# Waiting for a quarter of a weight block instead of the whole block, in a two-block float32 model kernel

## What is computed

```python
# first block
p = h @ w_in                       # "in": 11 weight blocks
...                                # RWKV recurrence, 31-tap convolution
mix = concat([rwkv_out, c]) @ w_out          # "out": 4 blocks
hid = h @ ffn_up                   # "up": 22 blocks, then a 3-tap convolution
f = (gelu(gate) * up) @ ffn_down   # "down": 12 blocks
# second block, layer 0 (latent attention, 512 tokens and 256 context tokens)
q_lat, kv_lat, k_pe, gate = split(t @ w_in)  # "mla_in": 7 blocks
q = (rms_norm(q_lat) @ w_qb)
kv = (rms_norm(kv_lat) @ w_kvb)    # "mla": 4 blocks
...                                # attention of 16 heads, then "mla_out": 4 blocks
# second block, layer 1 (differential attention): "diff" 16 blocks, "diff_out" 4 blocks
```

## Time and profile before

| | us |
|---|---|
| median of 3 runs | 1885.46 |
| lowest, highest | 1881.81, 1889.06 |
| the profiled execution | 1880.98 |
| its span on the core | 1879.2 |
| PE busy | 1767.7 (94%) |
| POOL busy | 961.4 (51%) |
| DVE busy | 1039.4 (55%) |

### The profile page before, as it was taken

One profiled execution on the slowest core, in us unless ns is written; L12 is line 12 of the kernel. 1 busy time (PEld: TensorE's weight loads), 2 busy tenths in 40 slices (PEclk: granted clock), 3 DMA queues, 4 the chain that ended last, 5 costly groups with the idle time before them and its releaser, 6 DMA issues.

```text
span 1879.2 us, 24128 instructions
## 1 busy us (share of the span) xinstructions
PE 1767.7 (94%) x9332; PEld 1398.8 (74%) x9332; DVE 1039.4 (55%) x1285; ACT 749.5 (40%) x1217; POOL 961.4 (51%) x762
## 2 busy tenths in 40 slices
PE   4999999999999999999898899999988999999977
PEld 2777999766578888886687677777846888888766
DVE  4498545366655555102453666666565666666565
ACT  3453767313233333001331565555134444444442
POOL 4353667365179999888155121234623444444062
PEclk8999999799999999999999999999999999999988
DMA  4121000133212232322211100002130111111121
GB/s 180 47 102 54 2 1 2 47 135 135 90 67 89 91 110 89 147 100 104 110 45 50 40 23 1 23 1 90 68 140 29 45 45 47 61 51 46 46 90 45
DMA packets 18715, 126.20 MB, mean 67 GB/s; under 512 B 2080, under 2 KB 2208, under 8 KB 4160
## 3 DMA queue, kind: packets, MB, share of 16 engines
q1 hardware_dynamic: 18048, 121.79, 17.6%
q10 hardware_dynamic: 576, 3.15, 0.5%
HBM read 122.83 MB, written 2.10 MB: 66 GB/s over the span
## 4 chain that ended last, share of the span: by engine, by line
PE 54%; issue 18%; POOL 14%; DVE 9%; ACT 3%; DMA 1%; POOLq 0%; SPq 0%; ACTq 0%; DVEq 0%
POOL w_hi L613 7%; PE banks L1152 4%; POOL cacc L637 4%; PE banks L1131 3%; PE banks L1312 3%; PE banks L1315 3%; PE banks L1313 3%; POOL w_lo L604 3%; PE banks L1013 3%; PE banks L720 3%; PE banks L1018 3%; PE banks L1014 3%; PE banks L1367 2%; PE banks L705 2%; PE banks L707 2%
## 5 line engine op out<-in xcount | busy, mean ns | idle before, releaser
L613 POOL TENSOR_TENSOR w_hi<-raw,der 128x512 fp32r<-128x512 f32 x300 | 347.0, 1167 | 547.5 <-PE banks L1315 210.6
L604 POOL TENSOR_TENSOR w_lo<-raw,w_hi 128x512 fp32r<-128x512 f32 x336 | 470.4, 1412 | 68.1 <-ACT w_hi L1440 68.1
L705 PE MATMUL banks<-h_hi,w_hi 128*128 128x512 f32 x528 | 210.1, 398 | 15.1 <-DVE h_lo L2016 12.6
L707 PE MATMUL banks<-h_hi,w_lo 128*128 128x512 f32 x528 | 206.5, 391 | 0.0
L706 PE MATMUL banks<-h_lo,w_hi 128*128 128x512 f32 x528 | 206.5, 391 | 0.0
L1312 PE MATMUL banks<-h_hi,w_hi 128*128 128x512 f32 (+1 forms) x384 | 147.0, 383 | 4.6 <-DVE h_lo L2496 3.9
L705 PEld LDWEIGHTS banks<-h_hi,w_hi 128*128 128x128 f32 x528 | 99.6, 189 | 43.5 <-issue 12.8
L1313 PE MATMUL banks<-h_lo,w_hi 128*128 128x512 f32 (+1 forms) x384 | 131.1, 356 | 0.0
L1915 ACT ACTIVATE dP<-banks,der 128x768 f32<-128x768 f32 x64 | 57.8, 902 | 167.9 <-DVE der L2529 167.9
L1315 PE MATMUL banks<-h_hi,w_lo 128*128 128x512 f32 (+1 forms) x384 | 116.4, 357 | 0.0
L707 PEld LDWEIGHTS banks<-h_hi,w_lo 128*128 128x128 f32 x528 | 99.7, 189 | 20.9
(11 more groups left out here) (455 smaller groups left out, 4231.1 us busy)
## 6 DMA issues: line engine op xcount, KB each, us to landing
raw<-in_stream SPq DMA_DIRECT2D x84, 1024.0 KB, 4.8
ada_raw<-in_ada_w SPq DMA_DIRECT2D x18, 1024.0 KB, 6.0
raw<-in_ada_w SPq DMA_DIRECT2D x6, 1024.0 KB, 4.8
xT<-in_x_t SPq DMA_DIRECT2D x2, 1024.0 KB, 6.0
xT<-in_x_t SPq DMA_DIRECT2D x1, 2048.0 KB, 7.8
out_t<-z SPq DMA_DIRECT2D x8, 256.0 KB, 2.0
ctxT<-in_ctx_t ACTq DMA_DIRECT2D x1, 1024.0 KB, 4.9
rope<-in_ropes ACTq DMA_DIRECT2D x2, 512.0 KB, 4.3
```

The costliest lines, as they stand in the source:

```text
L604: return pool.tensor_tensor(lo[:, h, part(i), :], raw_tiles(half)[:, part(i), :], hi[:, h, part(i), :], ALU.subtract)
L613: pool.tensor_tensor(hi[:, h, part(i), :], raw_tiles(half)[:, part(i), :], one, ALU.mult).then_inc(hi_done, 1)
L705: pe.matmul(banks[b][:, :], hi, rhs_hi[:, k, :], start=(at_k == 0), stop=False)
L707: mm = pe.matmul(banks[b][:, :], lo, rhs_hi[:, k, :], start=False, stop=(at_k == KT - 1))
```

## The change

A new semaphore `quarter_split` counts the low parts 0, 1 and 2 of every block, three a block. The last low part still counts `split_full`. The function `quarter(n, i)` gives the semaphore and the value that say that quarter i of block n is split. In `project`, the down loop and `mla_in` the wait for `split_full` of the block is replaced by four waits, one ahead of every fourth tile. All other products wait as before. So that the number of semaphores stays in bounds, `lam_exp` of the second layer now reuses `cln_root` with an offset of 1.

```diff
+    quarter_split = sem("quarter_split")
+    def quarter(n, i):
+        return (quarter_split, (PARTS - 1) * n + (i + 1)) if i < PARTS - 1 else (split_full, n + 1)
...
     # POOL, split()
-                    low_of(half, h, i - 1, hi, lo)
+                    low_of(half, h, i - 1, hi, lo).then_inc(quarter_split, 1)
...
     # POOL, input blocks 2 to 10
             for i in range(PARTS):
-                ins = low_of(half_of(n), half_of(n), i)
-            ins.then_inc(split_full, 1)
+                low_of(half_of(n), half_of(n), i).then_inc(quarter_split if i < PARTS - 1 else split_full, 1)
...
     # PE, project()
-            pe.wait_ge(split_full, n + 1)
             for j in range(2):
...
+                    if at_k % 4 == 0:
+                        pe.wait_ge(*quarter(n, 2 * j + at_k // 4))
...
     # PE, down loop
-                pe.wait_ge(split_full, 6 * i + (STREAM["down"] + u + 1))
                 for t in range(TILES):
...
+                    if t % 4 == 0:
+                        pe.wait_ge(*quarter(6 * i + (STREAM["down"] + u), t // 4))
...
     # PE, mla_in()
-                if m % 2 == 0:
-                    pe.wait_ge(split_full, n + 1)
...
-            mm = wide_project(0, 0, KT, m % 2, half_of(n), h2_hi, h2_lo, tile0=KT * (m % 2), ready=None if m else mh_ready, part=part)
+            for k in range(KT) if part is None else part:
+                if k % 4 == 0:
+                    pe.wait_ge(*quarter(n, 2 * (m % 2) + k // 4))
+                mm = wide_project(0, 0, KT, m % 2, half_of(n), h2_hi, h2_lo, tile0=KT * (m % 2), ready=None if m else mh_ready, part=[k])
```

More of the change, by code:

```diff
@@ L469, in build @@
     NL, LAM = 88, 96
-    lam_prod, lam_sum, lam_exp = (sem(n) for n in ("lam_prod", "lam_sum", "lam_exp"))
+    lam_prod, lam_sum = sem("lam_prod"), sem("lam_sum")
+    lam_exp = Later(cln_root, 1)
     o_sq, o_root, o_scaled = (sem(n) for n in ("o_sq", "o_root", "o_scaled"))
@@ L1871, in _ @@
         act.wait_ge(lam_sum, 1)
-        act.activation(der[:, LAM + 2:LAM + 4], banks[4][:, 0:2], ACT.Exp).then_inc(lam_exp, 1)
+        act.activation(der[:, LAM + 2:LAM + 4], banks[4][:, 0:2], ACT.Exp).then_inc(lam_exp.sem, 1)
         low_rows, high_rows = slice(0, 64), slice(64, 128)
@@ L2498, in _ @@
         dve.tensor_tensor(h2_lo[:, KT - 1, :], zh[:, 1, :], h2_hi[:, KT - 1, :], ALU.subtract).then_inc(mh_ready, 1)
-        dve.wait_ge(lam_exp, 1)
+        dve.wait_ge(*lam_exp.at(1))
         chain.link(dve.tensor_scalar(der[:, LAM + 4:LAM + 5], der[:, LAM + 3:LAM + 4], der[:, LAM + 2:LAM + 3], None, ALU.subtract))
```

## The result

The changed kernel takes 1874.36 us (median of 8 runs, 1867.35 to 1878.40) where the kernel before takes 1887.89 (8 runs, 1881.81 to 1889.37). The ratio is 0.993, with an interval of 0.9915 to 0.9945: faster by 0.7%, and the whole interval lies beyond 0.5%. The profiled executions took 1868.69 and 1880.98 us, 12.3 less; the sum of the prediction was 12.5.

The account below looks back on a forecast made before the run. PE bounds the kernel (busy 94% of the span), so only its waits for `w_lo` can go: 4.1 + 6.8 + 1.6 = 12.5 us off the median 1885.46 gives 1873.0 us, range 1867 to 1882.

Parts of the forecast that it names:

- Up and input projection, 0: In the 22 up and 11 input projection blocks PE was not held by POOL's split, so the gain is 0.
- Down projection, 4.1 us: PE's three gaps behind short blocks go whole, with the slow matmul after each: 1.22 + 1.34 + 1.22 + 0.3 us.
- the middle gap: Down projection, at 817.68: 1.34 us counted to POOL's pass, though the view of waits names ACT's queue.
- POOL keeps up: Down projection: three POOL passes take 28 us against PE's 30.0 us for three blocks, so PE runs through.
- The wait at `mla_in(10)`, 6.8 us: End of the latent input projection: the first piece needs only quarter 0, starting at 1000.63 instead of 1007.45.
- The clock behind it, 1.6 us: First tiles of `mla_in(10)`: without PE's idle time they run at full instead of half clock, 1.6 us more won.
- no idle time, no fall: At `mla_in(10)`: without PE's idle time the clock has no cause to fall to half; worth 1.6 us.
- The added waits, 0: 149 more wait executions on PE cost 0, because its queue runs ahead of the matmuls; upper bound 28 us.
- The stall behind `mla_in(11)` moves up and does not shrink: The stall of some 11 us (1033 to 1044.38) starts with DVE's fills after PE's last product and keeps its length.
- Rival (a): The 6.8 + 1.6 us are given back before 1044 through unmoved DVE or POOL work: 1881.4 us; chance 0.13.
- Rival (b), the clock: Half clock stays or moves behind the stall at 1033 to 1044: gain 9.3 us, time 1876.2; chance 0.13.
- The median, 1873.0: Whole kernel: the median of 1885.46 us falls by 12.5 us, 0.66% less; chance 0.65.

Follow-up runs that it names:

- the third experiment: Only the input and up projections wait by quarters, the signals on POOL stay, against the kernel before: 1887.14 us (10 runs), ratio 1.0.
- the first experiment: Only the down projection waits by quarters, the signals on POOL stay, against the kernel before: 1885.32 us (10 runs), ratio 0.9983.
- 3.0 us of idle time: Only the latent input projection waits in parts, by halves of a block instead of the whole block as in the kernel before: 1885.58 us in one run.

## Why the prediction was right, step by step

- **Up and input projection, 0.** Right: 10.88 us a block before and after, and the third experiment at a ratio of 1.0.
- **Down projection, 4.1 us.** Right: 4.2 in the trace (1.22, 1.34, 1.22 at the three gaps, and 0.1 for each slow matmul), 3.2 by the runs with this part alone, whose interval holds 4.1; in that kernel's profile 1.0 us goes to the longer half clock behind the wait at `mla_in(10)`. That the middle gap was POOL's and not ACT's was argued ahead and is shown by the first experiment. POOL keeps up: no late quarter shows in PE's waits.
- **The wait at `mla_in(10)`, 6.8 us.** Right: 10.65 - 3.92 = 6.7, with PE 0.14 behind quarter 0 instead of the 0.06 that were taken.
- **The clock behind it, 1.6 us.** Right in size: 12.23 - 10.65 = 1.6. (The 1.06 us that the prediction calls the fourth tile's is the third's.) That the size fits is in part luck: behind the same wait the clock cost 2.6 us in the profile with the down projection alone. The reason given (no idle time, no fall) holds at this place, and with 3.0 us of idle time left the fall and the whole loss were still there. As a general reason it fails: near 67 us the clock fell without idle time.
- **The added waits, 0.** Right, and far from the edge: in the input and up projections 48 waits a block instead of 4 cost nothing.
- **The stall behind `mla_in(11)` moves up and does not shrink.** Right to 0.02 us (-12.25 before it, -12.27 at 1044). Rival (a) fails: nothing in the stall hangs on work that did not move. What the prediction had wrong is what PE waits for first there: ACT's row, not DVE's fills.
- **Rival (b), the clock.** It did happen, but for other sums than it priced. The stretches lie elsewhere in after (one at 896.7, one at 1023.0, where before they were at 881.1 and 1038.1), and the largest effect was one that the prediction did not see. The stretch behind the stall costs nothing more in after, though it is twice as long. The modulation products behind the down projection ran at full clock in after, so that PE was 6.96 and then 7.9 us ahead, and then it waited (PE and DVE of after, and DVE of before):

```profile
898.29 0.77 PE L1021 MATMUL banks<-h_hi,w_hi 128*128 128x512 f32 x1 [3.69 <-DVE h_lo L2317]
...
897.18 0.96 DVE L2317 TENSOR_TENSOR h_lo<-mh,h_hi 128x768 fp32r<-128x768 f32 x1 [0.98 <-ACT h_hi L1667]
...
901.05 0.96 DVE L2308 TENSOR_TENSOR h_lo<-mh,h_hi 128x768 fp32r<-128x768 f32 x1 [0.99 <-ACT h_hi L1658]
```

  `h_lo` comes 897.18 - 901.05 = -3.87 us against before, what the down projection had won (3.86), and `mla_in(0)` starts with it. DVE's chain sets this place, so what the clock gave to PE in it is given back, in full. A step for the half clock at 881 would have been worth nothing in the sum, in either direction.
- **The median, 1873.0.** 1874.36 was measured. The sum was set against 1885.46, the median of three runs; further runs of that kernel have medians of 1885.6 to 1887.9. Against 1887.89 the sum gives 1875.4, and the difference of the medians is 13.5 us (10.4 to 16.0 by the interval). That the two profiled executions differ by 12.3 is closer than it can be relied on: behind 1400 the difference moves between 10.9 and 13.0 us with the clock.

Open: why the early stretch falls in some executions and not in others, and what the kernel would win if it never came. Whether the 32 and 96 rows bring it is not shown either: two profiles without it, where it falls in seven of twelve, may be chance.

## What to carry to other kernels

Where one engine prepares a block in pieces and another waits for the whole, read the gap at each block start: a gap of 1 us is worth a signal per piece, a near tie in the chain is worth nothing, and further waits that are met in time cost nothing on an engine whose queue has work. Price a removed wait together with the half clock behind it, but do not count on that while some us of the wait are left, expect its size to differ from one profile to the next (1.6 and 2.6 us here), and then look for the next engine's chain at which what was won is given back. Work taken off a critical place belongs into holes of its engine that the timeline shows; moved as one piece to "later" it became the next wait. And an edit that is to keep the clock up has a price of its own, to be read from matmuls at full clock in both kernels.

## What the runs showed of the hardware

- 990 more satisfied waits in the up loop, one ahead of each of 48 matmuls a block, left the starts at 0.226 to 0.227 us.
- The clock fell to half while PE had work without a break: from about 67 us in seven profiles of twelve, in the stretch of products that use 32 or 96 of 128 rows. None of the seven has a gap of PE between 46 and 90 us. This timeline of PE in the profile with the latent part alone shows two products of one form at full and at half clock:

```profile
63.60 1.12 PE L737 MATMUL banks<-Q,gup 96*128 96x512 f32 x2
...
66.82 2.07 PE L737 MATMUL banks<-Q,gup 96*128 96x512 f32 x2
```

  The Trainium skill, "TensorE: Matmul & The Clock Gate", section "HAM oscillation — how this bites in real kernels", names idle gaps of PE as what brings the fall; these traces show a fall without any. Against the profile of before what follows is 6.5 us later behind it (80.03 against 86.89, where it was 60.02 against 60.41 ahead of it). Of the changed kernel the execution without it took 1868.69 us and the one with it 1875.99; 4.9 us of these 7.3 arise at the stretch, so it may be a large part of the spread between runs.
- In the one profile with 3.0 us of idle time at `mla_in(10)` the clock fell, and it fell after work had begun again (clock 1.00 in the idle window, 0.50 in the one behind it).
- Two products with 32 rows each, on different rows, started at the same time and took 1.13 us together in the changed kernel; one alone took 1.12 us where full tiles stood between them.
